# Sample attention in four column tiles of TensorE, with three key slots and four value slots

## The chip, the cores and the metric

The kernel runs on one core of a Trainium2 chip. The metric is the time of the core on the device, in microseconds. One launch computes everything; the host only lays out arrays.

## What is computed

The reference is one layer of a decoder that mixes attention and a short convolution. Cut to what matters here:

```python
q, k, v, g_att, gb, gc, hh, g_conv = split(x @ w_in)     # x: 512 prompt rows, 8 samples of 8 rows
# attention over 8 heads of 64; per query three dilated windows (128,1), (512,4), (2048,16),
# merged by their softmax denominators; samples also read a cache of 2048 keys and values
att = o_att * silu(g_att)
u = gc * hh                                              # width-3 causal convolution
z = gb * conv3(u) * silu(g_conv)
y = layer_norm(alpha * x + concat(att, z) @ w_out)
new_k, new_v = last 2048 rows of cache + new rows        # the caches are outputs too
```

The merged branches are one softmax in which a key counts as often as it lies in a window; the masks hold the logarithm of that count. Of the 2048 cached positions 1280 are ever read (10 tiles of 128); the rest is only copied to the output.

## The kernel before

All matmuls of the projections are three products of fp32r halves (x_hi, x_lo, w_hi, w_lo), 24 instructions for half a tile of 288 tokens (`project`, L795 to L797); the sample attention runs in fp32. The engines' programs are written out by hand, each in the order in which it runs, with semaphores between them.

**Stages.** First 12 tiles of q, k and v are projected. Then come four rounds (`pe_round(i)`), each with five more tiles (`t0` to `t0 + 4`: c, h, b and the two gates), the prompt attention of one pair of heads, and the sample attention of one pair of samples with all eight heads. Then the output projection and the layer norm, over four tiles of 128 prompt rows and one of the samples. A round on PE is, in order: four times `prompt_scores`, `prompt_values`, `sample_scores(i, u)`, half a projection and `prompt_turn` (transposes); a half projection, `sample_turn` with a half projection in it; `sample_values(i, 0)` and `(i, 1)`; `project(t0 + 3, 0)`; `sample_values` 2 and 3; `project(t0 + 3, 1)`; `sample_values` 4; `project(t0 + 4, 0)`; `sample_out_turn`, the first `prompt_scores` of the next round, `project(t0 + 4, 1)`. In the last round `sample_values` 4 comes behind both halves of `t0 + 4`.

**Sample attention.** `q_bd` holds the queries of two samples with zeros around them: for each pair of heads 128 columns, 64 for each sample, of which 16 are filled. A piece of keys is a quarter of the 1280 positions, 320, for two samples and four pairs of heads: 2560 floats a partition. `sample_scores` (L886) multiplies one piece in eight matmuls of 128 rows by 64 columns over 320 keys; each sample has its own column tile of 64 in the bank `sc`, and the four pairs of heads add up in it, as the zeros keep them apart. The last piece adds eight matmuls over the 64 new tokens (L906). `mask_sample` (DVE, L615) adds the mask and writes `p_s`; then come a maximum, an exponential over 1344 columns (ACT, L428), the normalisation (L703), transposes into `pt_s` (L920), and the values: `sample_values(i, s)` (L925) takes two pieces of values, one for each sample, each of 256 positions by 512 features, in four matmuls of 64 columns over 512 (L937); `s = 4` adds the new tokens (L944). ACT copies `sc` into `o_s` (L448), PE turns it (L953), and ACT picks the blocks that belong to a head into `att_s`.

**What sets the order around it.** SP issues every load, in program order, and waits in that order. `load_w` (L203) fills one of two slots and waits for DVE's split of the tile two before. `load_k` (L210) fills one of two slots of 1280 KB, `load_v` (L218) one of six slots of 512 KB; both wait for the use of what is in the slot. In a round SP issues, in this order: w `t0+2`, w `t0+3`, k (i,2), k (i,3), w `t0+4`, k (i+1,0), w `t0+5`, k (i+1,1), w `t0+6`, v (i,6) to v (i,9), v (i+1,0) to v (i+1,5). In the last round the eight pieces of the output weights (`wo_raw`, L280) are loaded with v 6, 7 ahead of the fourth of them and v 8, 9 ahead of the sixth. ACT issues the copies of the caches, DRAM to DRAM, between its own work: `copy_k` (L374) and `copy_v` (L379) at fixed places of a round, one `copy_k` right behind the exponential that follows `project(t0 + 3, 0)`. DVE's order at the end of a round is a gate (`gate_half`, L625 to L637), the masks of the next prompt scores, the second gate, the split of w (L559), then the normalisation (L604) for which the next `prompt_turn` (L865) waits.

```python
def load_v(i, n):
    n += V_PIECES * i
    slot = n % V_SLOTS
    if n >= V_SLOTS:
        sp.wait_ge(v_used, n - V_SLOTS + 1)
```

## Time and profile before

| | |
|---|---|
| runs | 425.25 us median of 3 (423.67 to 425.73) |
| the profiled execution | 424.56 us, its span 422.8 us |
| PE busy | 93% of the span |
| DVE, ACT, POOL busy | 47%, 28%, 3% |
| DMA | 141.09 MB, mean 334 GB/s |
| TensorE's granted clock | 0.98 in the mean |

The span runs from the first to the last instruction; the time of an execution has 1.8 us more around it. PE is TensorE's matmuls, PEld its weight loads, SPq and ACTq the sequencers that issue DMAs. Matmuls overlap each other, so a group's busy time is the time that it covers, and the mean duration of one is longer than its share. A granted clock of 1.00 is 2.4 GHz, 0.50 is 1.2 GHz. "MATMUL 128*64 128x320" is a matmul with weights of 128 rows by 64 columns and 320 moving columns. A row by window gives its bounds and length, then the busy us (and instructions) of PE, PEld, DVE, ACT and POOL, the granted clock, the share of the DMA engines' time and their GB/s. A DMA share of 1.00 means that the core's 16 DMA engines worked all the time.

### The profile page before, as it was taken

To read this page: it belongs to the slowest core of one execution; us is meant where nothing else is said; L and a number is where in the kernel's file an instruction comes from. 1 tells how busy PE (TensorE), PEld (TensorE's weight loads), DVE (VectorE), ACT (ScalarE), POOL (GpSimd) and SP (SyncE) were. 2 spreads that over 40 slices of the span, in tenths; PEclk is the share of its full clock that TensorE was granted. 3 is DMA by queue.
4 is the path that set the end of the run, shared out by engine and by line. 5 is a ranking of instruction groups with operands and counts; after the bars stand their busy time and mean duration, and the time that the engine had idled before them with its cause. 6 is when DMAs were issued, how large, how long until landed. Compare 5 with 4: busy or idle time off the path is not lost.

```text
span 422.8 us, 6599 instructions
## 1 busy us (share of the span) xinstructions
PE 393.4 (93%) x2752; PEld 318.9 (75%) x2752; DVE 199.4 (47%) x369; ACT 118.9 (28%) x234; POOL 13.1 (3%) x32
## 2 busy tenths in 40 slices
PE   1999999979999999999899999999999999799991
PEld 1999999977787777787577788577779586588850
DVE  3522322324335376335367436358245688465554
ACT  4422222324333025333024334023434532310000
POOL 0000001000001000002000002000000002000000
PEclk9999999989999999999999999999999999789997
DMA  8999999869998994999993999993999893499996
GB/s 282 403 399 421 394 323 348 292 231 366 365 423 322 400 378 151 412 395 359 416 366 138 400 393 367 407 401 117 404 397 304 347 379 109 166 295 346 340 352 242
DMA packets 33967, 141.09 MB, mean 334 GB/s; under 512 B 3281, under 2 KB 3537, under 8 KB 31761
## 3 DMA queue, kind: packets, MB, share of 16 engines
q1 hardware_dynamic: 17618, 73.56, 45.6%
q10 hardware_dynamic: 16320, 67.11, 43.6%
q8 instruction: 22, 0.36, 0.3%
q14 instruction: 7, 0.06, 0.0%
HBM read 135.90 MB, written 71.86 MB: 491 GB/s over the span
## 4 chain that ended last, share of the span: by engine, by line
PE 79%; DVE 10%; DMA 5%; ACT 4%; issue 1%; ACTq 1%; SPq 1%
PE pj_b L795 8%; PE pj_b L797 7%; PE pj_b L796 7%; PE pj_a L795 7%; PE sc L899 7%; PE pj_a L797 7%; PE pj_a L796 6%; PE sc L937 6%; DVE rg L627 3%; DMA v_buf<-in_v_used 3%; PE po L881 3%; PE px L1023 3%; PE px L1024 3%; PE px L1025 3%; PE pt L865 2%; PE px L846 2%
## 5 line engine op out<-in xcount | busy, mean ns | idle before, releaser
L795 PE MATMUL pj_a<-x_hi,w_hi 128*128 128x288 f32 x256 | 78.1, 305 | 9.0 <-DVE x_lo L566 8.8
L795 PE MATMUL pj_b<-x_hi,w_hi 128*128 128x288 f32 x256 | 78.0, 305 | 0.7 <-DVE mix L637 0.7
L797 PE MATMUL pj_b<-x_hi,w_lo 128*128 128x288 f32 x256 | 76.0, 297 | 0.0
L796 PE MATMUL pj_b<-x_lo,w_hi 128*128 128x288 f32 x256 | 76.0, 297 | 0.0
L797 PE MATMUL pj_a<-x_hi,w_lo 128*128 128x288 f32 x256 | 75.7, 296 | 0.0
L796 PE MATMUL pj_a<-x_lo,w_hi 128*128 128x288 f32 x256 | 75.7, 296 | 0.0
L795 PEld LDWEIGHTS pj_a<-x_hi,w_hi 128*128 128x128 f32 x256 | 48.5, 190 | 19.2 <-issue 10.0
L559 DVE TENSOR_TENSOR w_lo<-w_raw,w_hi 128x1024 fp32r<-128x1024 f32 x32 | 39.2, 1226 | 36.0 <-ACT w_hi L352 36.0
L795 PEld LDWEIGHTS pj_b<-x_hi,w_hi 128*128 128x128 f32 x256 | 48.4, 189 | 6.7 <-issue 5.2
L796 PEld LDWEIGHTS pj_a<-x_lo,w_hi 128*128 128x128 f32 x256 | 48.5, 190 | 0.0
L797 PEld LDWEIGHTS pj_a<-x_hi,w_lo 128*128 128x128 f32 x256 | 48.5, 189 | 0.0
L796 PEld LDWEIGHTS pj_b<-x_lo,w_hi 128*128 128x128 f32 x256 | 48.5, 189 | 0.0
L797 PEld LDWEIGHTS pj_b<-x_hi,w_lo 128*128 128x128 f32 x256 | 48.4, 189 | 0.0
L352 ACT CAST w_hi<-w_raw 128x1024 fp32r<-128x1024 f32 x32 | 33.6, 1049 | 44.5 <-PE pj_b L797 41.9
L937 PE MATMUL sc<-v_buf,pt_s 128*64 128x512 f32 x160 | 37.4, 601 | 2.0 <-DMA v_buf<-in_v_used 2.0
L899 PE MATMUL sc<-k_buf,q_bd 128*64 128x320 f32 x256 | 37.6, 435 | 0.0
L627 DVE RECIPROCAL rg<-rg 128x288 f32<-128x288 f32 x16 | 31.3, 1953 | 0.6
L899 PEld LDWEIGHTS sc<-k_buf,q_bd 128*64 128x64 f32 x256 | 17.7, 138 | 12.9 <-issue 0.9
L937 PEld LDWEIGHTS sc<-v_buf,pt_s 128*64 128x64 f32 x160 | 10.4, 136 | 20.5 <-issue 19.4
L625 DVE TENSOR_SCALAR rg<-rg 128x288 f32<-128x288 f32 x16 | 5.0, 309 | 42.4 <-ACT rg L424 42.4
L409 ACT ACTIVATE p_pr<-p_pr,stat 128x512 f32<-128x512 f32 (+3 forms) x32 | 17.7, 554 | 22.6 <-DVE stat L592 22.6
L592 DVE CUSTOM_DVE_ANT_0 p_pr<-px,mask_pr 128x512 f32<-128x512 f32 (+3 forms) x32 | 14.4, 487 | 11.0 <-PE px L846 11.0
(118 smaller groups left out, 451.7 us busy)
## 6 DMA issues: line engine op xcount, KB each, us to landing
k_buf<-in_k_used SPq DMA_DIRECT2D x16, 1280.0 KB, 9.8
v_buf<-in_v_used SPq DMA_DIRECT2D x40, 512.0 KB, 7.2
out_k_used_out<-in_k_used ACTq DMA_DIRECT2D x16, 1280.0 KB, 11.1
out_v_used_out<-in_v_used ACTq DMA_DIRECT2D x20, 1024.0 KB, 14.4
w_raw<-in_w_tiles SPq DMA_DIRECT2D x32, 512.0 KB, 6.2
out_k_rest_out<-in_k_rest ACTq DMA_DIRECT2D x12, 1024.0 KB, 10.3
out_v_rest_out<-in_v_rest ACTq DMA_DIRECT2D x12, 1024.0 KB, 12.6
wo_raw<-in_w_out SPq DMA_DIRECT2D x8, 512.0 KB, 7.8
```

What stands on the lines that cost most here:

```text
L352: nc.scalar.copy(w_hi[:, c], w_raw[:, c]).then_inc(w_hi_done, 1)
L409: nc.scalar.activation(p, p, ACT.Exp, bias=negmax_pr[:, e:e + 1], scale=-1.0, accum_out=sum_pr[:, e:e + 1]).then_inc(pr_exp, 1)
L559: nc.vector.tensor_tensor(w_lo[:, c], w_raw[:, c], w_hi[:, c].bitcast(F32), ALU.subtract)\
L592: nc.vector.tensor_tensor_reduce(out=p_pr[:, e * SEQ:e * SEQ + w], in0=px[e][:, 0:w], in1=mask_pr[:, SEQ - w:], scale=-SCALE, scalar=BIG, ...
L627: nc.vector.reciprocal(rg[:, c], rg[:, c]).then_inc(g_step, 1)
L795: nc.tensor.matmul(out, w_hi[:, w], x_hi[:, c], start=(k == 0), stop=False)
L796: nc.tensor.matmul(out, w_hi[:, w], x_lo[:, c], start=False, stop=False)
L797: return nc.tensor.matmul(out, w_lo[:, w], x_hi[:, c], start=False, stop=(k == KT - 1))
L881: last = nc.tensor.matmul(po[e * 64:e * 64 + 64, t * P:(t + 1) * P], v_rows[:, v:v + 64], pt_pr[:, e * SEQ + k * P:e * SEQ + (k + 1) * P], ...
L899: last = nc.tensor.matmul(sc[b * 64:b * 64 + 64, 0:K_COLS], q, k_buf[:, k0:k0 + K_COLS], start=(hp == 0), stop=(hp == NHP - 1 and c < K_PI ...
L937: last = nc.tensor.matmul(sc[b * 64:b * 64 + 64, :], pt_s[:, t * P + b * 64:t * P + b * 64 + 64], v_buf[:, v0:v0 + 512], start=(t == 0), s ...
L1023: nc.tensor.matmul(out, x_hi[:, tok], wo[:, hi], start=(n == 0), stop=False)
```

## The change

A round now takes one pair of heads and all eight samples, where it took two samples and all heads. `q_bd` has a block of 32 columns for each sample, so a tile of the scores has four column tiles of 32, each with two samples that add up in it. A piece of keys is 320 positions of the pair of heads for eight samples (again 2560 floats a partition), in eight matmuls of 32 columns over 320. A piece of values is 128 positions for eight samples, in eight matmuls of 32 columns over 128, ten pieces a round, each with its own call of `sample_values`; the new tokens take eight matmuls over 128. The outputs of a round fill 256 columns of `sc`, so two transposes do for four and the copy into `o_s` is half as wide. `mask_new` and POOL's copy of it go; its columns are the same in all rounds and lie in `mask_s`. The bytes loaded and copied stay as they are, but for that mask.

The ring of keys has three slots, that of the values four. K (0,2) is loaded in the projections. In a round SP's order is w `t0+2`, w `t0+3`, k (i,3), w `t0+4`, k (i+1,0), w `t0+5`, k (i+1,1), w `t0+6`, v (i,4) to v (i,7), k (i+1,2), v (i,8), v (i,9), v (i+1,0) to v (i+1,3). On PE, pieces 0 to 3 of the values stand ahead of `project(t0 + 3, 0)`, 4 to 7 behind it, 8 and 9 behind `project(t0 + 3, 1)` (in the last round behind both halves of `t0 + 4`).

```diff
@@ -37,9 +37,10 @@
 S_COLS = USED + NS
 K_PIECES = 4
 K_COLS = USED // K_PIECES
-K_SLOT = NHP * 2 * K_COLS
+K_SLOT = DEC_BATCH * K_COLS
 V_PIECES = 10
-V_SLOTS = 6
+V_SLOTS = 4
+K_SLOTS = 3
 QT = SEQ // P
 X_CHUNKS = ((0, 1), (1, 3), (3, 5), (5, 7), (7, 8))
 PAD_COLS = 2 + SEQ + DEC_BATCH * (2 + DEC_SEQ)
...
@@ -97,20 +98,19 @@
-        k_buf = sb("k_buf", [P, 2 * K_SLOT], stack=early)
+        k_buf = sb("k_buf", [P, K_SLOTS * K_SLOT], stack=early)
-        q_bd = sb("q_bd", [P, NHP * P], stack=early)
-        mask_new = sb("mask_new", [P, NPAIR * NS], stack=early)
+        q_bd = sb("q_bd", [P, DEC_BATCH * 32], stack=early)
         v_buf = sb("v_buf", [P, V_SLOTS * 1024], stack=early)
-        o_s = sb("o_s", [P, D_ATT], stack=early)
+        o_s = sb("o_s", [P, 2 * P], stack=early)
...
@@ -205,10 +207,11 @@
             def load_k(i, c):
                 n = K_PIECES * i + c
-                if n >= 2:
-                    sp.wait_ge(k_used, n - 1)
-                sp.dma_start(k_buf[:, n % 2 * K_SLOT:(n % 2 + 1) * K_SLOT],
-                             d["k_used"][n * P:(n + 1) * P, :]).then_inc(k_in[n % 2], 16)
+                slot = n % K_SLOTS
+                if n >= K_SLOTS:
+                    sp.wait_ge(k_used, n - K_SLOTS + 1)
+                sp.dma_start(k_buf[:, slot * K_SLOT:(slot + 1) * K_SLOT],
+                             d["k_used"][n * P:(n + 1) * P, :]).then_inc(k_in[slot], 16)
             def load_v(i, n):
                 n += V_PIECES * i
...
@@ -236,8 +238,10 @@
                     load_k(0, 0)
                 if tile == 5:
                     load_k(0, 1)
-                if tile >= 6:
-                    load_v(0, tile - 6)
+                if tile == 7:
+                    load_k(0, 2)
+                if tile >= 8:
+                    load_v(0, tile - 8)
             load_w(QKV_TILES)
             load_w(QKV_TILES + 1)
...
@@ -255,7 +259,6 @@
                 last = i == NPAIR - 1
                 load_w(t0 + 2)
                 load_w(t0 + 3)
-                load_k(i, 2)
                 load_k(i, 3)
                 load_w(t0 + 4)
                 if not last:
...
@@ -263,9 +266,12 @@
                     load_w(t0 + 5)
                     load_k(i + 1, 1)
                     load_w(t0 + 6)
-                    for n in range(6, 10):
+                    for n in range(4, 8):
                         load_v(i, n)
-                    for n in range(0, 6):
+                    load_k(i + 1, 2)
+                    for n in range(8, 10):
+                        load_v(i, n)
+                    for n in range(0, 4):
                         load_v(i + 1, n)
...
@@ -273,7 +279,7 @@
             sp.wait_ge(k_used, K_PIECES * NPAIR)
             sp.wait_ge(s_masked, K_PIECES * NPAIR)
             sp.wait_ge(pr_pv, QT * NPAIR)
-            v_before = {3: (6, 7), 5: (8, 9)}
+            v_before = {2: (4, 5), 4: (6, 7), 6: (8, 9)}
             for n in range(KT):
                 for v in v_before.get(n, ()):
                     load_v(NPAIR - 1, v)
...
@@ -315,14 +321,10 @@
                 if i:
                     pool.wait_ge(k_used, K_PIECES * i)
                 for e in range(2):
-                    src = qk[e * 64:e * 64 + 64, 0:NHP * NT].rearrange("p (h t) -> p h t", t=NT)[
-                        :, :, SEQ + 16 * i:SEQ + 16 * i + 16].rearrange("p h (b q) -> p h b q", b=2)
+                    src = qk[e * 64:e * 64 + 64, i * NT + SEQ:(i + 1) * NT].rearrange(
+                        "p (r b q) -> p r b q", b=2, q=DEC_SEQ)
                     pool.tensor_copy(qbd_copy_ap(e), src).then_inc(qbd_done, 1)
                     pool.wait_ge(qbd_done, 2 * i + e + 1)
-                if i:
-                    pool.wait_ge(s_masked, K_PIECES * i)
-                pool.tensor_copy(mask_s[:, USED:], mask_new[:, i * NS:(i + 1) * NS]).then_inc(masked_new, 1)
-                pool.wait_ge(masked_new, i + 1)
                 if i:
                     pool.wait_ge(y_done, i)
                 pool.tensor_copy(u_s[:, :, 0:2], state[:, i * 2 * DEC_BATCH:(i + 1) * 2 * DEC_BATCH]
...
@@ -445,13 +447,13 @@
             def out_sample(i):
                 act.wait_ge(s_pv, i + 1)
-                nc.scalar.copy(o_s[:, :], sc[:, :]).then_inc(s_out, 1)
+                nc.scalar.copy(o_s[:, :], sc[:, 0:2 * P]).then_inc(s_out, 1)
             def out_sample_turned(i):
                 act.wait_ge(so_turned, i + 1)
...
@@ -885,27 +886,29 @@
             def sample_scores(i, c):
                 n = K_PIECES * i + c
-                pe.wait_ge(k_in[n % 2], 16 * (n // 2 + 1))
+                pe.wait_ge(k_in[n % K_SLOTS], 16 * (n // K_SLOTS + 1))
                 if c == 0:
                     pe.wait_ge(qbd_done, 2 * (i + 1))
                     if i:
                         pe.wait_ge(s_out, i)
                 if n:
                     pe.wait_ge(s_masked, n)
-                for hp in range(NHP):
+                ends = c == K_PIECES - 1
+                for b in range(2):
+                    for r in range(NPAIR):
+                        q = q_bd[:, (2 * r + b) * 32:(2 * r + b + 1) * 32]
+                        k0 = n % K_SLOTS * K_SLOT + (2 * r + b) * K_COLS
+                        last = nc.tensor.matmul(sc[r * 32:r * 32 + 32, 0:K_COLS], q, k_buf[:, k0:k0 + K_COLS],
+                                                start=(b == 0), stop=(b == 1 and not ends), skip_group_check=True)
+                if ends:
                     for b in range(2):
-                        q = q_bd[:, hp * P + b * 64:hp * P + b * 64 + 64]
-                        k0 = n % 2 * K_SLOT + (2 * hp + b) * K_COLS
-                        last = nc.tensor.matmul(sc[b * 64:b * 64 + 64, 0:K_COLS], q, k_buf[:, k0:k0 + K_COLS],
-                                                start=(hp == 0), stop=(hp == NHP - 1 and c < K_PIECES - 1),
-                                                skip_group_check=True)
-                if c == K_PIECES - 1:
-                    for hp in range(NHP):
-                        for b in range(2):
-                            q = q_bd[:, hp * P + b * 64:hp * P + b * 64 + 64]
-                            last = nc.tensor.matmul(sc[b * 64:b * 64 + 64, K_COLS:K_COLS + NS], q,
-                                                    qk[:, (NHP + hp) * NT + SEQ:(NHP + hp + 1) * NT],
-                                                    start=False, stop=(hp == NHP - 1), skip_group_check=True)
+                        for r in range(NPAIR):
+                            q = q_bd[:, (2 * r + b) * 32:(2 * r + b + 1) * 32]
+                            last = nc.tensor.matmul(sc[r * 32:r * 32 + 32, K_COLS:K_COLS + NS], q,
+                                                    qk[:, (NHP + i) * NT + SEQ:(NHP + i + 1) * NT],
+                                                    start=False, stop=(b == 1), skip_group_check=True)
                 last.then_inc(k_used, 1)
             def sample_turn(i, g):
...
@@ -922,35 +925,35 @@
                     last = nc.tensor.transpose(bank_[0:NS, 256:384], p_s[:, USED:], ident[:, :])
                 last.then_inc(s_turned, 1)
-            def sample_values(i, s):
-                pe.wait_ge(s_moved, 4 * i + (s // 2 + 1 if s < V_PIECES // 2 - 1 else 4))
-                if s == 0:
+            def sample_values(i, t):
+                n = V_PIECES * i + t
+                ends = t == V_PIECES - 1
+                pe.wait_ge(s_moved, 4 * i + (t // 4 + 1 if not ends else 4))
+                if t == 0:
                     pe.wait_ge(s_masked, K_PIECES * (i + 1))
+                pe.wait_ge(v_in[n % V_SLOTS], 16 * (n // V_SLOTS + 1))
                 for b in range(2):
-                    n = V_PIECES * i + 2 * s + b
-                    pe.wait_ge(v_in[n % V_SLOTS], 16 * (n // V_SLOTS + 1))
-                for half in range(2):
+                    for r in range(NPAIR):
+                        v0 = n % V_SLOTS * 1024 + (2 * r + b) * P
+                        last = nc.tensor.matmul(sc[r * 32:r * 32 + 32, b * P:(b + 1) * P],
+                                                pt_s[:, t * P + r * 32:t * P + r * 32 + 32], v_buf[:, v0:v0 + P],
+                                                start=(t == 0 and b == 0), stop=False, skip_group_check=True)
+                last.then_inc(v_used, 1)
+                if ends:
                     for b in range(2):
-                        n = V_PIECES * i + 2 * s + b
-                        t = 2 * s + half
-                        v0 = n % V_SLOTS * 1024 + half * 512
-                        last = nc.tensor.matmul(sc[b * 64:b * 64 + 64, :],
-                                                pt_s[:, t * P + b * 64:t * P + b * 64 + 64],
-                                                v_buf[:, v0:v0 + 512], start=(t == 0), stop=False)
-                        if half == 1:
-                            last.then_inc(v_used, 1)
-                if s == V_PIECES // 2 - 1:
-                    for b in range(2):
-                        last = nc.tensor.matmul(sc[b * 64:b * 64 + 64, :],
-                                                pt_s[0:NS, USED + b * 64:USED + b * 64 + 64],
-                                                v_new[:, :], start=False, stop=True)
+                        for r in range(NPAIR):
+                            last = nc.tensor.matmul(sc[r * 32:r * 32 + 32, b * P:(b + 1) * P],
+                                                    pt_s[0:NS, USED + r * 32:USED + r * 32 + 32],
+                                                    v_new[:, i * P:(i + 1) * P], start=False, stop=True,
+                                                    skip_group_check=True)
                     last.then_inc(s_pv, 1)
             def sample_out_turn(i):
                 pe.wait_ge(s_out, i + 1)
                 pe.wait_ge(s_moved, 4 * (i + 1))
-                for hp in range(NHP):
-                    last = nc.tensor.transpose(pt[0][:, hp * P:(hp + 1) * P], o_s[:, hp * P:(hp + 1) * P], ident[:, :])
+                for b in range(2):
+                    last = nc.tensor.transpose(pt[0][:, b * P:(b + 1) * P], o_s[:, b * P:(b + 1) * P], ident[:, :])
                 last.then_inc(so_turned, 1)
             def pe_round(i):
...
@@ -976,13 +979,18 @@
                 sample_turn(i, 2)
                 sample_values(i, 0)
                 sample_values(i, 1)
-                project(t0 + 3, 0)
                 sample_values(i, 2)
                 sample_values(i, 3)
+                project(t0 + 3, 0)
+                sample_values(i, 4)
+                sample_values(i, 5)
+                sample_values(i, 6)
+                sample_values(i, 7)
                 pe.wait_ge(z_done, i + 1)
                 project(t0 + 3, 1)
                 if not last:
-                    sample_values(i, 4)
+                    sample_values(i, 8)
+                    sample_values(i, 9)
                     project(t0 + 4, 0)
                     sample_out_turn(i)
                     prompt_scores(i + 1, 0)
...
```

## Rows read from the trace of the kernel before

**Rows 1.** The page: busy time of each engine

```profile
PE 393.4 (93%) x2752; PEld 318.9 (75%) x2752; DVE 199.4 (47%) x369; ACT 118.9 (28%) x234; POOL 13.1 (3%) x32
```

**Rows 2.** Groups of instructions by form, PE: busy us, mean ns, idle before

```profile
L937 PE MATMUL sc<-v_buf,pt_s 128*64 128x512 f32 x160 | 37.4, 601 | 2.0 <-DMA v_buf<-in_v_used 2.0
...
L899 PE MATMUL sc<-k_buf,q_bd 128*64 128x320 f32 x256 | 37.6, 435 | 0.0
...
L944 PE MATMUL sc<-v_new,pt_s 64*64 64x512 f32 x16 | 4.3, 614 | 0.0
```

**Rows 3.** The chain of waits, start of round 1: start us, us, what

```profile
153.99 0.42 ACT rg L424
...
163.57 1.13 DVE w_lo L559
...
165.35 1.09 PE pt L865 x8
...
183.18 2.15 PE sc L899 x16
...
185.33 0.47 PE sc L906 x16
```

**Rows 4.** Busy time by window, with granted clock, DMA share and GB/s

```profile
155.40:165.35 9.95, 9.13 (x66) 7.47 (x64) 8.33 (x15) 3.27 (x7) 0.00 (x0) 1.00 0.41 156
...
165.35:197.44 32.09, 31.99 (x280) 26.91 (x280) 14.07 (x43) 11.84 (x29) 2.44 (x6) 1.00 1.00 383
...
207.50:215.70 8.20, 8.20 (x45) 4.52 (x45) 3.10 (x5) 1.34 (x2) 0.00 (x0) 1.00 1.02 416
```

**Rows 5.** Timeline of SP's queue in round 1: start us, us, what

```profile
165.10 5.76 SPq L210 DMA_DIRECT2D k_buf<-in_k_used  x2
...
193.88 0.43 SPq L210 DMA_DIRECT2D k_buf<-in_k_used  x1
...
199.60 0.33 SPq L203 DMA_DIRECT2D w_raw<-in_w_tiles  x1
...
199.97 15.55 SPq L218 DMA_DIRECT2D v_buf<-in_v_used  x10
```

**Rows 6.** The chain of waits, values of round 1

```profile
207.50 1.94 PE sc L937 x8
...
215.70 0.33 PE pj_a L795
```

**Rows 7.** Timeline of PE's weight loads in the values of round 1

```profile
197.92 0.14 PEld L937 LDWEIGHTS sc<-v_buf,pt_s 128*64 128x64 f32 x2 [0.28 <-issue]
198.35 0.14 PEld L937 LDWEIGHTS sc<-v_buf,pt_s 128*64 128x64 f32 x2 [0.29 <-issue]
```

**Rows 8.** DMA issues: count, KB each, median us from issue to landing

```profile
k_buf<-in_k_used SPq DMA_DIRECT2D x16, 1280.0 KB, 9.8
v_buf<-in_v_used SPq DMA_DIRECT2D x40, 512.0 KB, 7.2
```

**Rows 9.** Landing of the k_buf loads issued at 193.9 and 130.2 us, in turn

```profile
DMA to landing us min/median/max: 9.7/9.7/9.7
...
DMA to landing us min/median/max: 7.3/7.3/7.3
```

**Rows 10.** The chain of waits: values of round 0, then of round 3

```profile
149.59 1.00 PE sc L944 x4
...
327.29 3.58 PE sc L937 x16
351.37 0.43 PE px L1023
```

**Rows 11.** Busy time by window, columns as above: two stretches after PE idled

```profile
93.10:95.60 2.50, 2.50 (x19) 2.08 (x20) 0.48 (x2) 0.59 (x1) 0.00 (x0) 0.50 0.67 238
...
362.70:366.10 3.40, 0.51 (x5) 0.27 (x3) 1.31 (x2) 2.44 (x4) 0.00 (x0) 0.88 0.41 119
...
366.10:372.10 6.00, 5.94 (x14) 4.71 (x15) 5.19 (x8) 2.17 (x3) 0.00 (x0) 0.50 1.02 349
```

49 lines of the change are left out of this document (23 added, 26 removed).

## The prediction

> **What bounds the kernel now.** I read four views in this order. The page first: PE is busy 393.4 of 422.8 us [rows 1], and in the rounds the DMA engines are nearly always busy as well [rows 4]. So both must be followed, and a cut on PE counts only where no transfer and no other engine ends the wait behind it. Then the groups of instructions: scores (L899) cover 37.6 us of PE, values (L937) 37.4 us, their new-token part (L944) 4.3 us [rows 2]. That is all that column tiles can shorten. Then the chain of waits and the SP queue through round 1, which I lay out now, and last the windows, for the rate of the DMA engines and the clock.
>
> Round 1 has three stages. (a) **Its start is not PE's.** After the last-but-one projection of round 0, ACT's exponential at 153.99 opens a chain of ACT and DVE (gates, softmax, the split of w at 163.57) that ends at the transposes of 165.35 [rows 3]; PE, ahead of them, was busy 9.13 of 9.95 us [rows 4]. The first scores of the round lie beside this chain. The same split lets SP's next loads go: K pieces from 165.10 [rows 5]. (b) **From 165.35 to the values at 197.44** PE works through, 31.99 us busy in 32.09, with three sets of scores in it, and the DMA engines are as full: share 1.00, 383 GB/s [rows 4]. (c) **The values**, from 197.44 to the projection at 215.70. SP issues the last-but-one K piece at 193.88, w at 199.60, and from 199.97 ten V pieces [rows 5]; the engines are full at 416 GB/s [rows 4], and PE waits at 207.50 for a V piece of the second pair [rows 6]. So this stage has almost no slack in transfers already, with six slots.
>
> **The change, part by part.**
>
> Scores. A set of 16 records takes 2.15 us [rows 3], 0.27 us for each two. L937 holds 160 records for 80 matmuls of the code (20 a round), so one matmul is two records. Weight loads come two by two, 0.43 us apart [rows 7], which is what one 512-column record streams: two records run at once, one per column tile. With four tiles, as many matmuls of 320 columns stay, and a set has four steps in place of eight: 1.08 us instead of 2.15. No row shows four at once. Bounds: 2.15 us (two at once stay, no gain) and 1.08. I take 1.08, since two tiles reach their full factor of two. The new-token part (16 records of 64 columns, 0.47 us [rows 3]) takes 29 ns a record already; I leave it. Sixteen sets give 17 us of PE time in all.
>
> Values. 80 matmuls of 128 columns a round and 8 for the new tokens replace 20 and 2 of 512: as many columns, four times the records. A 128-column record streams a quarter of 0.43 us, 0.107; four at once are 0.45 us for a V piece of 16 records, 4.5 us for ten instead of 8.6, and 0.45 instead of 0.97 for the new part. That asks for a record every 27 ns, where the L906 rows show 29; bounds are 0.43 and 0.9 us a piece (two at once). I take 0.45.
>
> Small things. Two transposes fewer (L953), a shorter o_s copy on ACT, one POOL copy and one small DMA less: they lie beside (a)'s chain or ahead of the first round's waiting tiles, so nothing, but 0.2 us in the tail, where PE waits for what follows these transposes. If (a)'s chain ended sooner, they would be worth 0.2 us a round. K (0,2) now loads in the projections before round 0, in the time of two V pieces: nothing.
>
> What the transfers do. A V piece is 0.52 MB, a K piece 1.31 MB [rows 8]; at 0.41 MB/us these are 1.28 and 3.2 us. In stage (b) K (i,2) is there already, which takes 3.2 us of transfers out; PE's three sets are 3.24 us shorter. The two cancel: against the start A of the values (197.44 before) the K piece issued at 193.88 lands where it did, at A + 6.1 (9.7 us after its issue [rows 9]). Behind it in SP's queue stand, in the new order, w, V 4 to 7, **K (i+1,2)**, V 8, V 9: 0.52 + 2.10 + 1.31 + 1.05 = 4.98 MB, 12.1 us. ACT's copy of a K piece, issued after the first values, takes another 3.2 us out of the same engines. So V 9 lands at A + 21.4; with its own 0.45, the new part's 0.45 and 0.3 to drain, the next projection starts at A + 22.5. Before it was A + 18.2 (215.70 [rows 6]). PE would be there at A + 11, but with four slots V 4 can't be asked for until V 0 is used, and must pass the queue. A V slot's wait on SP also holds SP's K (i+1,2) and the V pieces of the next round; these come some 4 us later and find the idle DMA time at the round's start, so no one waits for them.
>
> **The sum.**
> - Rounds 1 and 2: -3.24 (three sets; the first set's 1.08 is lost in (a)) + 4.3 = +1.1 each, +2.2.
> - Round 0 has no such chain ahead, so four sets count, -4.3. Its K piece is issued at 130.2 and lands 7.3 later [rows 9], now 3.2 sooner, at 134.3; + 15.3 + 1.2 = 150.8, against the end of L944 at 150.6 [rows 10]: +0.2.
> - Round 3 loads the output weights, two pieces between each two of V. V 6 and 7 land near A + 10.2 and 12.8; then two projections, one gate (3.7 us) and one more projection, V 8, 9 and the new part: A + 25.4 against 351.37 - 327.2 = 24.15 [rows 10]. With -3.24: -2.0.
> - The clock. During V 4 to 7 PE is busy some 0.45 us in 1.3 or more, for 9 us. The trace shows what follows such a stretch: after 3.4 us with 0.51 busy the granted clock was 0.50 (1.2 GHz) for 6.0 us of full work, and for 2.5 us from 93.1 [rows 11]. That costs 1.3 to 3.0 us of work. In rounds 0 to 2 the wait for V 9 covers 2 us of it, so 0.3 each (bounds 0 and 1.4); in round 3 nothing covers it: 1.1.
> - Tail: -0.2.
>
> 0.2 + 2.2 - 2.0 + 0.9 + 1.1 - 0.2 = **+2.2 us**. The profiled execution took 424.56 us (span 422.8); the median of the runs shown is 425.25, so I say 427.4 for it. About 0.5% (2.1 us) is what a measurement of this kernel can tell from no change; the forecast lies on that edge. Some 30 us of PE's work go, and PE waits for V instead.
>
> **Rivals.**
>
> *Two at once stay (15%).* Nothing in the rows shows a third tile at work, and the two records of a matmul need the same tile. If the records start strictly in order, the second record of tile 0 holds back tile 1, and four tiles run like two. Then scores keep their 2.15 us and values 0.87 a piece, while V waits remain. Stage (b) isn't shorter, its K lands sooner, but w is only issued at A + 2.2: V 9 comes near A + 20, the projection at A + 22, +3.8 in rounds 1 and 2, +5 in round 0, +2.7 in round 3: +15, **440 us**. Against it: weight loads now come in pairs within the 0.43 us of the records before, which a strict order of a matmul's two records, one behind the other, wouldn't give. It decides from the first set: 2.1 us, not 1.1.
> The Trainium skill ("TensorE: Matmul & The Clock Gate", Part 3, What overlaps and what doesn't) says that matmuls start and end strictly in program order, and that weight loads overlap running matmuls only where the row group differs. Taken at its word it gives this rival. The trace disagrees with its half on weight loads: all 128 rows are in use and the loads still overlap.
>
> *Transfers fit better (17%).* ACT's K copy drains behind V 9, or the engines share in SP's favour: then V 9 lands 3.2 us earlier, each of rounds 0 to 2 is -3.0, -2.1, -2.1 and round 3 -3.5: **414.5 us**. For it: V pieces land a mere 7.2 us after issue in the median now [rows 8]. Against: the copy is issued while V 5 to 7 are still in the queue, and no row shows one queue going first.
>
> *PE's whole saving arrives (4%).* 13 sets (14.0) and four rounds of values (4.6 less, 18): 393 us. It would need the V slots to refill within 4 us of use; ten V pieces and one K piece in some 11 us are 590 GB/s, and the rows show 416 [rows 4].
>
> **How the numbers follow.** My forecast has 62%, spread over 422 to 433 by the clock's bounds (0 to 4 us over three rounds) and by 1 us a round on V 9's landing: 6% below 423.1, 28% within, 28% above. With 17% and 4% faster, 15% slower, 2% slower for things not seen (instruction fetch for 528 more matmul records and their loads): faster 27%, same 28%, slower 45%. The range runs from 413 to 437: it takes in the second rival and leaves out most of the first, and the third.
>
> **What would show it.** L899 a set 1.1 us and L937 0.45 a piece, with waits of PE for DMA v_buf grown from 2.0 us to over 25 us in total, in four places, V 5 to 7 and V 8, 9. The granted clock at 0.50 for some us in each round's values. DVE before the transposes of the round's start unchanged. From the round's first K load to V 9's landing about 51 us of full DMA engines, then a quiet stretch. I am wrong in kind if the PE wait for v_buf stays under 10 us, or a set still takes 2.1 us.

## The result and the profile after

The changed kernel takes **436.83 us** in the median of 4 runs (434.40 to 438.98), the kernel before 424.46 us on the same chip (4 runs, 423.34 to 425.73): ratio 1.030, 95% interval 1.026 to 1.035. So it is 3.0% slower where I had said 0.5%, just inside the upper end of my range (437.0). The profiled execution took 437.18 us, its span 435.4 us, against 422.8 before.

The page of the changed kernel: busy time of each engine, then from its 40 slices (tenths) those of PE and of the granted clock, then its groups of values and scores.

```profile
PE 373.1 (86%) x3272; PEld 324.0 (74%) x3272; DVE 198.7 (46%) x369; ACT 118.2 (27%) x234; POOL 10.5 (2%) x28
...
PE   2999999979995698998398999399899488799992
...
PEclk9999999989998598999689999679999979989998
...
L939 PE MATMUL sc<-v_buf,pt_s 128*32 128x128 f32 x640 | 28.1, 322 | 30.9 <-DMA v_buf<-in_v_used 30.9
...
L903 PE MATMUL sc<-k_buf,q_bd 128*32 128x320 f32 x256 | 21.6, 457 | 0.0
```

PE has 20 us less to do than in [rows 1]. The scores cover 21.6 us where they covered 37.6 [rows 2], with records as long as before (457 ns, then 435), so four of them run at once. But the idle time ahead of the values, ended by loads of v_buf, has grown from 2.0 us [rows 2] to 30.9. The dips in the PE line (one a round) stand beside dips of the clock line.

Three marks carry the rest: **A** is the first value matmul of a round, **P** the projection behind the new tokens' part (in the last round the output projection), **T** the first transposes of the next round. All three can be read off the timeline of PE.

| us, rounds 0 to 3 | T to A | A to P | P to next T | P of round 3 to the end |
|---|---|---|---|---|
| before | 32.8, 32.1, 32.1, 32.1 | 16.8, 18.2, 17.8, 24.1 | 14.8 each | 71.5 |
| after | 29.8, 30.5, 29.0, 29.0 | 24.5, 23.5, 24.0, 30.6 | 14.8 each | 69.3 |

Scores do what was promised (T to A), but for round 1, where T to A is 30.5 us. The whole loss lies in A to P, the stage of the values. Timeline of PE in that stage of round 1, the projections' records left out but for the first and the last of `pj_b` (start us, busy us, what, in brackets the idle time before and what ended it):

```profile
209.39 0.64 PE L939 MATMUL sc<-v_buf,pt_s 128*32 128x128 f32 x16 [3.82 <-DMA v_buf<-in_v_used]
210.65 1.08 PE L939 MATMUL sc<-v_buf,pt_s 128*32 128x128 f32 x16 [0.61 <-DMA v_buf<-in_v_used]
213.29 1.08 PE L939 MATMUL sc<-v_buf,pt_s 128*32 128x128 f32 x16 [1.56 <-DMA v_buf<-in_v_used]
216.26 1.08 PE L939 MATMUL sc<-v_buf,pt_s 128*32 128x128 f32 x16 [1.89 <-DMA v_buf<-in_v_used]
217.27 0.61 PE L796 MATMUL pj_b<-x_hi,w_hi 128*128 128x288 f32 x1
...
222.00 0.29 PE L798 MATMUL pj_b<-x_hi,w_lo 128*128 128x288 f32 x1
222.22 1.08 PE L939 MATMUL sc<-v_buf,pt_s 128*32 128x128 f32 x32
223.23 0.64 PE L946 MATMUL sc<-v_new,pt_s 64*32 64x128 f32 x16
```

The reader is to see three things. V 4 and V 5 are 1.26 us apart, V 6 and V 7 2.64 and 2.97 us. The projection behind V 7 takes 4.95 us. And V 8 and 9 (222.22) had **no wait at all**: V 9 landed at 221.75, 0.47 us before PE was ready for V 8. My whole sum had that landing as what ends the stage.

Busy time by window in the same stage (A to V 4, V 4 to 7, from there to P; columns as in [rows 4]), and the landing of V 7 (first row) and V 9, us from issue:

```profile
200.30:209.39 9.09, 5.28 (x89) 4.88 (x89) 4.62 (x7) 1.68 (x4) 0.00 (x0) 1.00 0.95 367
209.39:217.27 7.88, 3.81 (x64) 2.34 (x65) 0.05 (x1) 0.00 (x0) 0.00 (x0) 0.57 1.02 423
217.27:223.80 6.53, 6.53 (x76) 5.97 (x72) 1.00 (x2) 1.35 (x2) 0.00 (x0) 0.73 0.77 313
```

```profile
DMA to landing us min/median/max: 11.1/11.1/11.1
...
DMA to landing us min/median/max: 10.0/10.0/10.0
```

The engines are full while the pieces come slowly (1.02, 423 GB/s), so something else is moved. It is ACT's copy of a key piece, issued in the middle of them (timeline of ACT's queue):

```profile
205.62 0.58 ACTq L376 DMA_DIRECT2D out_k_used_out<-in_k_used  x1
```

### The profile page after: what moved, and what is told of

The parts are those of the page before. It is cut to its first block, busy times and chain, and to the rows that moved or that the text cites. A ratio compares the mean times of both kernels' runs of the same rounds, so it can differ in the third digit from the quotient of the medians.

```text
span 435.4 us, 7646 instructions
## 1 busy us (share of the span) xinstructions
PE 373.1 (86%) x3272; PEld 324.0 (74%) x3272; DVE 198.7 (46%) x369; ACT 118.2 (27%) x234; POOL 10.5 (2%) x28
## 4 chain that ended last, share of the span: by engine, by line
PE 70%; DMA 12%; DVE 10%; ACT 4%; SPq 2%; issue 1%; ACTq 1%
DMA v_buf<-in_v_used 10%; PE pj_b L796 8%; PE pj_b L797 8%; PE pj_b L798 8%; PE pj_a L796 6%; PE pj_a L798 6%; PE pj_a L797 6%; PE sc L903 4%; DVE rg L628 3%; PE po L882 3%; PE px L1032 3%; PE px L1033 3%; PE px L1034 3%; PE sc L939 2%; PE pt L866 2%; DVE w_lo L561 2%
## 5 line engine op out<-in xcount | busy, mean ns | idle before, releaser
L796 PE MATMUL pj_b<-x_hi,w_hi 128*128 128x288 f32 x256 | 81.5, 318 | 0.7 <-DVE mix L638 0.7
L797 PE MATMUL pj_b<-x_lo,w_hi 128*128 128x288 f32 x256 | 79.1, 309 | 0.0
L796 PEld LDWEIGHTS pj_b<-x_hi,w_hi 128*128 128x128 f32 x256 | 51.7, 202 | 5.2 <-issue 3.6
L939 PE MATMUL sc<-v_buf,pt_s 128*32 128x128 f32 x640 | 28.1, 322 | 30.9 <-DMA v_buf<-in_v_used 30.9
L797 PEld LDWEIGHTS pj_b<-x_lo,w_hi 128*128 128x128 f32 x256 | 51.7, 202 | 0.0
L798 PEld LDWEIGHTS pj_b<-x_hi,w_lo 128*128 128x128 f32 x256 | 51.5, 201 | 0.0
L939 PEld LDWEIGHTS sc<-v_buf,pt_s 128*32 128x32 f32 x640 | 19.7, 125 | 37.6 <-issue 37.6
L354 ACT CAST w_hi<-w_raw 128x1024 fp32r<-128x1024 f32 x32 | 33.6, 1051 | 44.4 <-PE pj_b L798 41.9
L411 ACT ACTIVATE p_pr<-p_pr,stat 128x512 f32<-128x512 f32 (+3 forms) x32 | 17.7, 555 | 22.5 <-DVE stat L594 22.5
L903 PE MATMUL sc<-k_buf,q_bd 128*32 128x320 f32 x256 | 21.6, 457 | 0.0
L426 ACT ACTIVATE rg<-pj_b 128x288 f32<-128x288 f32 x8 | 3.3, 410 | 62.0 <-PE pj_b L798 61.9
L1032 PE MATMUL px<-wo,x_hi 128*128 128x512 f32 (+1 forms) x48 | 19.0, 396 | 1.1 <-issue 1.1
## 6 DMA issues: line engine op xcount, KB each, us to landing
out_v_used_out<-in_v_used ACTq DMA_DIRECT2D x20, 1024.0 KB, 12.6
out_k_rest_out<-in_k_rest ACTq DMA_DIRECT2D x12, 1024.0 KB, 10.1
wo_raw<-in_w_out SPq DMA_DIRECT2D x8, 512.0 KB, 10.1
```

What stands on the lines that cost most here:

```text
L354: nc.scalar.copy(w_hi[:, c], w_raw[:, c]).then_inc(w_hi_done, 1)
L411: nc.scalar.activation(p, p, ACT.Exp, bias=negmax_pr[:, e:e + 1], scale=-1.0, accum_out=sum_pr[:, e:e + 1]).then_inc(pr_exp, 1)
L796: nc.tensor.matmul(out, w_hi[:, w], x_hi[:, c], start=(k == 0), stop=False)
L797: nc.tensor.matmul(out, w_hi[:, w], x_lo[:, c], start=False, stop=False)
L798: return nc.tensor.matmul(out, w_lo[:, w], x_hi[:, c], start=False, stop=(k == KT - 1))
L903: last = nc.tensor.matmul(sc[r * 32:r * 32 + 32, 0:K_COLS], q, k_buf[:, k0:k0 + K_COLS], start=(b == 0), stop=(b == 1 and not ends), skip_ ...
```

## The experiments

Fifteen kernels ran. Unless a line says otherwise each is the changed kernel with one edit, timed beside the kernel before. "2/6" is two key and six value slots, "3/4" the changed kernel's rings.

**Tiles and rings apart.** The first two take the change in halves.

e1, four tiles with the old rings and the old load order (`pad` is a tile that nothing uses):

```diff
-V_SLOTS = 4
-K_SLOTS = 3
+V_SLOTS = 6
+K_SLOTS = 2
...
+        pad = sb("pad", [P, 512], stack=early)
...
```

> The four column tiles alone, with the old rings (two key slots, six value slots) and the old order of loads. Theory A (the tiles pay, the rings cost): V 6 to 9 are again the only value pieces that must arrive inside the values, PE waits for v_buf some 1 to 3 us a round, the clock stays at 1.00 in most rounds, and each round is about 3 us shorter than before the change: 411 to 415 us, ratio 0.97 to 0.98. Rival B (the tiles themselves cost, through 528 more matmul records, their instruction fetch or a DMA backlog in the shorter rounds): 424 us or more.

427.03 us, ratio 1.006 (1.002 to 1.010): not faster. Groups of e1, keys then values:

```profile
L900 PE MATMUL sc<-k_buf,q_bd 128*32 128x320 f32 x256 | 24.4, 506 | 9.1 <-DMA k_buf<-in_k_used 9.1
L936 PE MATMUL sc<-v_buf,pt_s 128*32 128x128 f32 x640 | 21.8, 279 | 11.2 <-DMA v_buf<-in_v_used 11.2
```

A key wait of 9.1 us that neither kernel has, and T to A of 36.4, 35.1 and 33.6 us in rounds 1 to 3. With two key slots K (i,2) can be asked for only when the round's first set of scores is done, and it stands behind w in SP's order: it is issued at 165.71 us in round 1, where the kernel before issued it at 165.10. This I had not foreseen. The traces show one thing more: it then takes 14.4 us to land (9.8 before), and the w ahead of it 10.0 (3.2 before). Queues of ACT and SP there, first the kernel before, then e1:

```profile
164.57 0.58 ACTq L374 DMA_DIRECT2D out_k_used_out<-in_k_used  x1
164.73 0.33 SPq L203 DMA_DIRECT2D w_raw<-in_w_tiles  x1
```

```profile
163.89 0.58 ACTq L373 DMA_DIRECT2D out_k_used_out<-in_k_used  x1
165.34 0.33 SPq L206 DMA_DIRECT2D w_raw<-in_w_tiles  x1
```

ACT issues that copy as soon as the half projection behind the round's first scores is done. Behind the shorter first set this is 1.4 us ahead of w, where it was 0.2, and PE then waits 3.0 us for K (1,2). No run moves these copies alone, so what part of the key wait is theirs and what part the ring's stays open.

e2, two column tiles with the new rings:

```diff
-V_SLOTS = 6
+V_SLOTS = 4
+K_SLOTS = 3
...
-            v_before = {3: (6, 7), 5: (8, 9)}
+            v_before = {2: (4, 5), 4: (6, 7), 6: (8, 9)}
...
```

> The old two column tiles with the new rings (three key slots, four value slots, the new order of loads). Theory A: scores stay at 2.15 us a set, but V 4 to 9 and a key piece must arrive inside the values, V 9 comes 20 us after the values' start, and PE waits: 434 to 441 us, ratio 1.025 to 1.04, with less time at half clock than in the changed kernel, since the values take twice as long on PE. Rival B: no more than 427 us, since PE is as busy as before.

455.71 us, ratio 1.075 (1.068 to 1.083). The direction is as expected, the size larger. T to A is that of before, A to P 24.3 to 25.1 us (32.4 in round 3). So on rings 3/4 the tiles are worth 19 us, and without the tiles the rings cost 31.

**What ends the stage.** e3 puts K (i+1,2) behind the next round's V 0 to 3, so that V 8 and 9 don't queue behind it.

```diff
-                    load_k(i + 1, 2)
                     for n in range(8, 10):
                         load_v(i, n)
                     for n in range(0, 4):
                         load_v(i + 1, n)
+                    load_k(i + 1, 2)
```

> The changed kernel with K (i+1,2) loaded behind the next round's V 0 to 3 in place of between V 7 and V 8. Theory A (V 7's landing and the half clock after it set the end of the values): V 9 lands 3.2 us earlier, but the projection ahead of it takes 5 us at half clock and hides that already: -0.5 us a round in three rounds, ratio to the kernel before 1.025 to 1.03 (435 us). Rival C (the queue up to V 9 sets it, as I predicted): 3.2 us less in each of rounds 0 to 2, 427 us, ratio 1.005.

436.41 us (435.00 to 436.98): nothing. V 9 lands at A + 18.4 to 19.2, some 3 us sooner, and A to P stays at 23.8 to 24.0. The timeline of PE says why (V 7, then V 8 and 9): V 7 comes as late as ever, and the projection between them runs at half clock.

```profile
213.80 1.08 PE L939 MATMUL sc<-v_buf,pt_s 128*32 128x128 f32 x16 [0.77 <-DMA v_buf<-in_v_used]
...
219.84 1.08 PE L939 MATMUL sc<-v_buf,pt_s 128*32 128x128 f32 x32
```

So V 9's landing by itself isn't what ends the stage; nor is it K (i+1,2) that makes V 7 late. e4 leaves the loads alone and keeps TensorE at work in the waits, with 37 dummy matmuls of 512 columns a round (16, 3, 8 and 10 before V 4 to V 7):

```diff
+            def keep_busy(i, count):
+                pe.wait_ge(pr_masked, 2 * QT * (i + 1))
+                for _ in range(count):
+                    nc.tensor.matmul(px[0][:, :], x_hi[:, 0:P], x_hi[:, 0:512], start=True, stop=True)
...
```

> The changed kernel with 37 matmuls of 512 columns more in each round's values, into a bank that nobody reads then: 16 ahead of V 4, 3 ahead of V 5, 8 ahead of V 6, 10 ahead of V 7, 0.22 us each, inside the waits for these pieces. Nothing of the result changes. Theory A (part of the loss is the clock): the granted clock stays at 1.00 in the values, the projection behind V 7 takes 3.1 us in place of 4.7 to 5.2, V 9's landing then ends the wait: -0.8 us a round in rounds 0 to 2, -1.5 us at the start of round 1, -3 us in round 3: 430 to 432 us, ratio 1.013 to 1.02. Rival D (the half clock is hidden behind transfers and costs nothing): 437 us or more.

437.56 us, ratio 1.030. The mean granted clock rose from 0.93 to 0.98 and the projection behind V 7 from 4.95 to 3.4 us, but A to P was still 22.4 to 24.1 in rounds 0 to 2 (23.5 to 24.5 in the changed kernel). V 9 landed at A + 21.1 to 22.7. Also, the 10 dummies before V 7 ran 2.56 us, to the start of V 7 at 216.91; V 7 had landed at 215.4. They stood in the way, so e4 alone settles nothing. e7 is e3 and e4 together:

> Both single edits at once: K (i+1,2) loaded behind the next round's V 0 to 3, and 37 dummy matmuls a round in the waits for V, which keep TensorE at work. Each alone left the time where it was (436.4 and 437.6 us). Theory A (two limits side by side, each about as long): together they pay, V 9 lands near A + 19 and is the only limit left, A to P is 20 us in rounds 0 to 2 (23.5 to 24.5 in the changed kernel), so 426 us, 424 to 429. Rival B (a third thing sets the projection's start, such as the gate that frees its bank): A to P stays above 22.5, 434 to 437.

435.70 us (433.27 to 441.60): Theory A's 426 is missed. Here too the dummies stood in the way: in round 1 V 7 landed at 214.8 and started at 219.3, behind 8 and 10 of them, and A to P was 27.5 us (22.8 and 21.7 in rounds 0 and 2). So e7 settles nothing either, and e15 below has fewer.

e8 moves V 8 and 9 behind the projection (t0+4, first half) and the next prompt scores; ACT's `out_sample` and `out_sample_turned` move back with them (not shown):

```diff
+                    project(t0 + 4, 0)
+                    prompt_scores(i + 1, 0)
                     sample_values(i, 8)
                     sample_values(i, 9)
-                    project(t0 + 4, 0)
+                    project(t0 + 4, 1)
                     sample_out_turn(i)
-                    prompt_scores(i + 1, 0)
-                    project(t0 + 4, 1)
```

> The changed kernel, with V 8 and V 9 of rounds 0 to 2 moved behind the projection (t0+4, first half) and the next round's first prompt scores; the turn of the sample output goes behind the second half. The bytes and their order stay. Theory A: the chain of ACT and DVE to the next round's first transposes (14.8 us) now starts from V 7 + the half-clock projection, A + 21.2, and no longer from V 9, A + 23.5: 2.3 us a round less, 430 us; V 9's landing at A + 21.5 is covered by the projection. Rival B (V 7 and the projection alone set the start, V 9 never did): no change, 436 us. Rival C (V 8 and 9 now delay the second half, whose gate ends the chain): 438 us or more.

436.29 us (435.40 to 440.25): nothing gained. From A to the next T it takes 38.7 to 40.1 us (after: 38.4 to 39.3). The trace is of the longest of the five executions, 440.25 us, and V 4 lands 2.7 and 5.3 us later in it in rounds 1 and 2 than after, so the us of rounds 1 and 2 can't be compared. The chain that ends at T needs the second half as well, and that now stands behind V 9. The traces bear this out: the second half starts 10.1 us ahead of T here, as it does after (10.15), while the first half starts 16.0 us ahead of T in round 0 where it is 14.8 after. Covering one of the two halves doesn't help: Rival C's mechanism, though not its price.

**The copy.** e5 moves one line of ACT's program, so that the copy of a key piece is issued behind the exponential after P:

```diff
                 exp_gate(i, 3, 0)
-                copy_k(i, 3)
...
                     exp_gate(i, 4, 0)
+                    copy_k(i, 3)
                     copy_v(i, 3)
```

> The changed kernel, with ACT's copy of a key piece (1.31 MB read and as much written, 3.2 us of all DMA engines) issued behind the exponential of the last gate of the round (after the projection that follows V 9) and not between V 4 and V 7. Theory A (two limits stand side by side: the landing of V 7 with the projection behind it at half clock, and the landing of V 9): the copy delays both, so without it V 7 lands at A + 13 (15.9 before) and V 9 at A + 18.5 (21.5), the stage from the first values to the projection takes 20 us and not 23.5 to 24.5, three times: 437 - 11 = 426 us. Rival B (the clock alone sets the stage): V 7 comes sooner, so 2 to 3 us a round too, but V 9 needn't: 429. Rival C (the copy only moves: it now runs beside the next round's w and keys, and delays K (i+1,3) or the first w): A to P is 3 to 4 us shorter and T to A as much longer: 436.

**422.03 us**, ratio 0.992 (0.989 to 0.995): 14.8 us less than the changed kernel, more than Theory A's 11. PE in the values of round 1, V 4 to V 9, and ACT's queue:

```profile
201.93 1.08 PE L940 MATMUL sc<-v_buf,pt_s 128*32 128x128 f32 x16 [3.78 <-DMA v_buf<-in_v_used]
203.18 1.08 PE L940 MATMUL sc<-v_buf,pt_s 128*32 128x128 f32 x16 [0.17 <-DMA v_buf<-in_v_used]
204.46 1.08 PE L940 MATMUL sc<-v_buf,pt_s 128*32 128x128 f32 x16 [0.20 <-DMA v_buf<-in_v_used]
205.73 1.08 PE L940 MATMUL sc<-v_buf,pt_s 128*32 128x128 f32 x16 [0.20 <-DMA v_buf<-in_v_used]
...
211.95 1.08 PE L940 MATMUL sc<-v_buf,pt_s 128*32 128x128 f32 x32
```

```profile
217.01 0.58 ACTq L376 DMA_DIRECT2D out_k_used_out<-in_k_used  x1
```

The pieces are 1.25 to 1.28 us apart throughout; V 7 lands 12.8 us behind A (15.9 in the changed kernel), V 9 at A + 18.4 (21.5). Both ends of the stage moved by 3.1 us and A to P went to 20.2, 20.7 and 21.1, in round 3 to 27.1 (30.6); T to A of round 1 went from 30.5 to 29.0, as no half clock falls on its start here. Together that is the 14.8 us. The copy had lain between V 5 and V 7. The next keys came in time (T to A 29.0 to 29.8), so Rival C falls.

e12 makes the same move in the kernel before.

> The kernel before with the same move of the copy alone: it tells whether the 13.5 us were the move's by itself or only the changed kernel's. Theory A (only where the values' loads end the wait): in the kernel before PE waits little for values, V 9's landing ends its stage at about A + 17, so it gains at most 2 to 3 us in rounds 0 to 2: 418 us, 415 to 422, so that the changed kernel with the copy moved (422) is no faster than this. Rival B (the copy costs nothing there, since six slots cover it): 425.

424.10 us, ratio 0.998 (0.994 to 1.002): nothing there, Rival B. With two tiles and six value slots the copy's place costs nothing; with four tiles it costs 14.8 us with four slots and, in e11 below, 4.8 with six.

e13 is e5 and e3 together.

> The changed kernel (3 key, 4 value slots) with the copy moved and K (i+1,2) behind the next round's V 0 to 3. With the copy moved, V 7 lands at A + 12.8 and V 9 at A + 18.5, with the projection at A + 20.7. Theory A (now V 9's landing alone sets the projection): V 9 lands 3 us earlier, but the projection behind V 7 at half clock (12.8 + 0.5 + 4.7 = 18.0, plus 1.6 for V 8, 9 and the new tokens) then sets it at A + 19.6: 1.1 us a round, 419 us. Rival B (as without the move of the copy, nothing at all): 422. Rival C (the key piece comes late for the next round's scores): T to A grows, 423 or more.

423.47 us (419.76 to 424.32) against 422.03. V 9 lands at A + 16.1, A to P is 19.3 to 19.5 us as Theory A says, but T to A is 30.6 in three rounds (29.0 with e5): the round's start runs for a while at half clock in this execution. What A to P gained, 0.8 to 1.6 us a round, T to A lost in three rounds (1.5 to 1.6), so the total can't tell what V 9's landing is worth now.

e15 adds fewer dummies than e4 to e13, meant to end before each landing:

```diff
+                for t, count in zip(range(4, 8), (0, 3, 18, 3) if last else (16, 3, 3, 3)):
+                    keep_busy(i, count)
+                    sample_values(i, t)
```

> The changed kernel with the copy moved and K (i+1,2) behind (423.5 us), plus dummy matmuls that keep TensorE at work in the waits for V, now short enough to end ahead of each piece: 16 before V 4 and 3 before each of V 5 to 7 (0.22 us each), in the last round 3 before V 5, 18 before V 6, 3 before V 7. In the first clock probe 8 and 10 of them stood before V 6 and V 7 and ran on past their landing, so it settled nothing. Theory A (half clock in the projection behind V 7 is the term that I had sized at 0.3 us a round): V 7 lands at A + 12.7 as before, the projection takes 3.1 us and not 4.7 to 5.2, and the half clock at the round's start (T to A 30.6, not 29.0) goes: 3 us a round, 414 us, 411 to 418. Rival B (V 9's landing at A + 16 takes over as the limit): A to P 18.0 and T to A 30.6: 419. Rival C (the clock is worth nothing): 423.

422.73 us (420.64 to 426.16), ratio to before 0.996, e13's 0.994: Rival C. Groups of the values in e13 and in e15, and e15's clock by slices:

```profile
L940 PE MATMUL sc<-v_buf,pt_s 128*32 128x128 f32 x640 | 28.6, 325 | 18.0 <-DMA v_buf<-in_v_used 17.9
```

```profile
PEclk9999999998999998999999999999999999999998
...
L940 PE MATMUL sc<-v_buf,pt_s 128*32 128x128 f32 x640 | 22.4, 276 | 3.6 <-DMA v_buf<-in_v_used 3.6
```

The half clock in the values is gone, and no time is won. That at the start of rounds 1 and 2 is still there (T to A 30.6). In the profiled executions of e13 and e15 V 7 and the projection behind it take 4.9 to 5.0 and 4.0 us in rounds 0 to 2, so only 1.0 us a round was to be had in the values; V 7 landed 0.5 to 1.6 us later in e15, and in round 1 the last dummies ran some 0.6 us past that.

**The trade.** e10 has three key slots and all six value slots. It is 1 MB more on chip than the changed kernel, and it fits.

```diff
-V_SLOTS = 4
+V_SLOTS = 6
...
-                    for n in range(4, 8):
-                        load_v(i, n)
-                    load_k(i + 1, 2)
-                    for n in range(8, 10):
+                    for n in range(6, 10):
                         load_v(i, n)
-                    for n in range(0, 4):
+                    load_k(i + 1, 2)
+                    for n in range(0, 6):
...
```

> Four column tiles with three key slots and all six value slots (1 MB more than the changed kernel), keys (i+1,2) behind V 9 in SP's order. The step on trial is the trade of two value slots for a key slot. Theory A (the four slots are what costs: the six pieces that can be asked for only after V 0 is used): only V 6 to 9 are loaded in the stage, V 9 lands at A + 13 to 14, and PE has V 4 and 5 at hand: A to P about 14 us (24 in the changed kernel, 18 before), T to A stays at 29 to 30 us: 10 us a round less than the changed kernel in rounds 0 to 2, some 5 in round 3: 402 us, 397 to 410, faster than both. Rival B (the transfers as a whole bound the round, 51 us of full engines plus what is not overlapped, and the keys come late instead, as with two key slots): T to A grows to 35, 418 us.

**411.51 us** (410.65 to 416.40), ratio 0.971 (0.964 to 0.978). Its groups of scores and values:

```profile
L903 PE MATMUL sc<-k_buf,q_bd 128*32 128x320 f32 x256 | 21.1, 449 | 0.0
...
L939 PE MATMUL sc<-v_buf,pt_s 128*32 128x128 f32 x640 | 22.3, 283 | 15.0 <-DMA v_buf<-in_v_used 15.0
```

No key wait, half the value wait; T to A 29.0 to 30.6, A to P 18.2 to 20.3 (21.3 in round 3). Against after that is 4 to 5 us less in rounds 0 to 2, not the 10 that I had expected, and 9 in the last: V 9 still lands at A + 16 to 16.8, since the copy lies between these four pieces too.

e11 is e10 with the copy moved.

> Three key slots, six value slots, four tiles (411.5 us so far), and ACT's copy of a key piece moved from between the value loads to behind the exponential of the last gate. Theory A (the copy shares the DMA engines with whatever SP has asked for: in the changed kernel its move was worth 13.5 us, V 7 landing at A + 12.8 and not 15.9): V 9 lands at A + 13.5 (16.0 to 16.8 with the copy in between), less half clock behind it, A to P 15.5 us and not 18 to 20: 4 us a round in rounds 0 to 2 and 2 to 3 in round 3: 398 us, 394 to 403. Rival B (with the values out of the way the round is bound by DMA work as a whole, 51 us of the 59 that it would take, so the copy now delays the keys or w): T to A grows by what A to P loses, 408 to 412.

**406.67 us**, ratio 0.957 (0.953 to 0.961), the fastest of all. 4.8 us less than e10, a bit over a third of Theory A's 13.5. The execution that was traced took 415.25 us, so I read no stages from it.

e16 is e11 with dummies before V 6 and V 7.

> Three key slots, six value slots, copy moved (406.7 us), plus 16 dummy matmuls before V 6 and 3 before V 7 (2 and 5 in the last round). Theory A (V 6, 7 land at A + 10.1 and 11.4, then a projection at half clock, then V 8, 9): with the full clock the projection ends at A + 15, V 9 has landed at A + 14, P at A + 16.8 and not 17.7 to 20, T to A 29.0 and not 30.6: 3 us a round, 399 us, 396 to 403. Rival C (the clock is worth nothing, transfers set all of it): 406.

408.40 us (407.57 to 409.56): Rival C, and if anything slower. A to P is 17.1 us in three rounds, with no wait for v_buf left. The dummies are in the path here too: V 6 landed at A + 9.0 to 9.3 and started at A + 10.1, V 7 at 10.5 to 10.8 and 11.6.

```profile
L940 PE MATMUL sc<-v_buf,pt_s 128*32 128x128 f32 x640 | 21.6, 276 | 0.0
```

e14 is the kernel before with rings 3/6 and e10's load order.

> The kernel before (two column tiles) with three key slots and six value slots and the load order of the 411.5 us kernel: what the third key slot is worth without the four tiles. Theory A (the four tiles are worth their PE work once neither ring holds it up: 3.2 us of scores and about 1.7 us of values where PE sets the end): this kernel is 13 to 18 us slower than 411.5, so it stays at 425 to 430, the third key slot alone gives nothing. Rival B (the key slot brings the gain, the tiles little): 411 to 416.

423.31 us, ratio 0.998 (0.994 to 1.001): without the tiles the third key slot is worth nothing. e6 is e1 with the copy moved.

> Four tiles with the old rings (two key, six value slots, 427.0 us) and the copy moved. Theory A (with two key slots K (i,2) and K (i,3) can be asked for only when the first scores of the round are done, and the four-tile scores come sooner than they land): T to A stays at 33 to 36 us and the time at 420 to 427: the copy isn't what makes the keys late. Rival B (the copies delayed the keys): T to A 30, 410 us.

422.59 us in the median of four runs that lie far apart (417.65, 420.24, 424.95, 426.15), ratio 0.986 with a wide interval (0.976 to 0.996), so its gain over e1 isn't measured well. The 410 of Rival B is far off, and T to A stays at 34.0 to 35.1 us in rounds 1 to 3: this copy isn't what makes the keys late. The copies at the round's start stand as in e1 (1.5 us ahead of w, K (1,2) lands 13.2 us after its issue). In e10, whose third slot already holds K (i,2), the copies stand there as well and no key is waited for: the slot is enough to cover it.

Medians, us, without and with the copy moved:

| | 2/6 | 3/4 | 3/6 |
|---|---|---|---|
| two column tiles | 424.5, 424.1 | 455.7, not tried | 423.3, not tried |
| four column tiles | 427.0, 422.6 | 436.8, 422.0 | 411.5, 406.7 |

## Why the prediction was wrong

**Right.** A set of scores runs four at once: T to A is 3.1 us shorter in rounds 2 and 3, as three sets of 1.08 said, and the *two at once* rival falls: its 440 us is nearer to the measured time than mine, but by luck. The timeline of PE shows one set and its new-token part:

```profile
187.13 1.28 PE L903 MATMUL sc<-k_buf,q_bd 128*32 128x320 f32 x16
188.23 0.41 PE L909 MATMUL sc<-qk,q_bd 128*32 128x64 f32 x16
```

16 records cover 1.1 us to the next row's start (2.15 in [rows 3]). A piece of values takes 0.4 to 0.5 us at full clock. The Trainium skill ("TensorE: Matmul & The Clock Gate", Part 3, What overlaps and what doesn't) has matmuls start and end in program order. The trace doesn't speak against that order (the records of the set start one behind the other, four within 0.02 us and the next four 0.27 to 0.29 us later); what it refutes is what the rival drew from it, that the second record of one tile holds back the next tile.

The first set's saving is lost at the round's start, as said: P to T is 14.8 us in both kernels. In round 0 it is lost too, which I had not said: A comes 3.2 us sooner (133.7 to 130.5), not 4.3; the sum went by the transfers there and didn't use it. V 9 lands at A + 21.5 in rounds 1 and 2 (said: 21.4), in part by luck: the K piece ahead of the values landed at A + 5.2, not 6.1, and what follows took 16.3 us, not 15.3.

**The step that failed** is the end of the values' stage: "So V 9 lands at A + 21.4; with its own 0.45, the new part's 0.45 and 0.3 to drain, the next projection starts at A + 22.5. [...] PE would be there at A + 11". PE was there at A + 22.0. I had added the copy's 3.2 us to V 9's landing alone and never worked out V 7's. The copy shares the engines from its issue (205.62), so V 6 and 7 come 2.6 to 3.0 us apart instead of 1.28; V 7 lands at A + 15.9, its own matmuls and the projection at half clock (4.95 us) follow, then V 8, V 9 and the new part, none of which is done beforehand: A + 23.5. e5 shows the first part (V 7 at 12.8), e3 that V 9's landing, 3 us sooner, changes nothing.

**The clock** was the second mis-sized term. I had 2.5 to 6.0 us of half clock a round, at a cost of 1.3 to 3.0 us that was mostly covered. It was 10 to 14 us in each of rounds 0 to 2 and 6.8 in round 3 (here that of round 0, columns as above), so that in rounds 0 to 2 the landings of V 5 to V 7 and most of the projection behind them fall into it.

```profile
138.90:152.60 13.70, 8.88 (x83) 7.26 (x84) 0.74 (x2) 0.00 (x0) 0.00 (x0) 0.50 1.01 414
169.60:173.00 3.40, 3.22 (x20) 2.89 (x20) 0.93 (x4) 1.17 (x2) 0.00 (x0) 0.50 0.99 331
```

The second row is the start of round 1, also at half clock (T to A 30.5, not 29.0). What it does to the work itself can be read: V 7 and the projection behind it take 6.0 to 6.4 us in rounds 0 to 2, and 4.0 in e4; T to A is 1.5 to 1.6 us longer where 3.4 us of its start are at half clock. But its price is not its length: e4, e15 and e16 restored the clock in the values and won nothing. At full clock the projection of round 1 would be done 1.6 us sooner, and PE would then wait for V 9 (221.75); from the rows above I estimate 0.9 us a round to be had at most. What the clock costs by itself stays open, since the dummies of e4, e7, e15 and e16 were in part in the path.

**The sum**, span against span (after less before, my terms in brackets, the clock's among them):
- To P of round 0: +4.4 (+0.5). K (1,1) was issued at 126.90 and took 9.3 us, where I had used 7.3 from [rows 9]; V 9 landed at 153.0, not 149.6.
- Round 1 +3.7 (+1.4), round 2 +3.1 (+1.4): the step above, and in round 1 the half clock at its start.
- Round 3: +3.4 (-0.9). V 6 and 7 landed at A + 12.1 and 15.0, I had 10.2 and 12.8. The same copy lies between them: with it moved this stage takes 27.1 us, not 30.6. Two projections and a gate stand behind V 7 and nothing covers them.
- Tail: -2.1 (-0.2). The trace of before has 6.8 us of half clock in it from 365.3, part of it in [rows 11], that of after 3.4 us. The change isn't needed for it: e12 and e14, with two tiles, have tails of 69.6 us.

Together +12.6 where I had +2.2 (both against the span). Of the 10.4 us between them 3.9 are round 0's, 2.3 and 1.7 those of rounds 1 and 2, and 4.3 round 3's; the tail takes 1.9 off.

**The rivals.** *Transfers fit better* named the right lever, the copy, but took it for luck. In the changed kernel it falls on the wrong side; moved by hand (e5) it gives 422.0, not 414.5. *PE's whole saving* falls.

**What the change is.** With the copies where they are, the four tiles need the third key slot (e1: 427.0, e10: 411.5) and the key slot needs the tiles (e14: 423.3). What spoils them is the pair of value slots given for it: 436.8 against 411.5, 25 us for 1 MB (422.0 against 406.7 with the copy moved). I took that trade as given and never worked out that both rings fit.

## What to carry to other kernels

Work out the landing of every piece that PE waits for, not only of the last: behind each stands its own work, and the stage ends with the later of the two sums. When two limits are about as long, an experiment that moves one alone shows nothing (e3); e5 moved both. A copy on another queue takes its share from the moment that it is issued, so its bytes belong to the pieces in flight then; it is one line to move. And before two buffers are traded, count whether both fit.
